# A decoder step on one core: the page loop directly behind the q, k, v projection, unrolled, with the memory projection in its first chunks

## The reference

```python
def sb_block(z, mask, v, carry):
    log_om = jnp.where(mask, jax.nn.log_sigmoid(-z), 0.0)
    suffix = lax.cumsum(log_om, axis=3, reverse=True) - log_om + carry[..., None]
    a = jnp.where(mask, jnp.exp(jax.nn.log_sigmoid(z) + suffix), 0.0)
    o = jnp.einsum("bhqk,bkhd->bqhd", a, v.astype(jnp.float32))
    return o, carry + jnp.sum(log_om, axis=3)

def sb_attention_sample(q, k_new, v_new, cache_k, cache_v, page_table, sb_bias):
    ...
    def page_step(state, phys):                 # 32 pages of 128 keys, newest first
        o_acc, carry = state
        kp = cache_k[phys]
        vp = cache_v[phys]
        zp = sb_logits(q, kp, sb_bias)
        o_p, carry = sb_block(zp, True, vp, carry)
        return (o_acc + o_p, carry), None
    (o, _), _ = lax.scan(page_step, (o, carry), page_table.T, reverse=True)

def memory_kv(mem, g_mem, w_ck, w_cv):          # 256 memory tokens, 1024 -> 512
    mn = rmsnorm(mem, g_mem)
    mk = (mn @ w_ck).reshape(b, N_MEM, CA_HEADS, CA_HEAD_DIM)
    mv = (mn @ w_cv).reshape(b, N_MEM, CA_HEADS, CA_HEAD_DIM)
```

## Time and profile before

| what | value |
|---|---|
| median of 3 runs | 1255.34 us |
| span of the profiled execution (no other time of its own is given) | 1264.7 us |
| TensorE busy in the span | 1122.9 us, 89% |
| VectorE, ScalarE, GpSimd busy | 646.5, 393.0, 405.4 us |
| end of the q, k, v projection on TensorE | 185.3 us |
| page loop, first to last score product | 237.75 to 622.31 us |
| output projection ends | 702.4 us |
| read from HBM | 206.18 MB |

### The profile page before, as it was taken

One profiled execution on the slowest core, in us unless ns is written; L12 is line 12 of the kernel. 1 busy time (PEld: TensorE's weight loads), 2 busy tenths in 40 slices (PEclk: granted clock), 3 DMA queues, 4 the chain that ended last, 5 costly groups with the idle time before them and its releaser, 6 DMA issues.

```text
span 1264.7 us, 27562 instructions
## 1 busy us (share of the span) xinstructions
PE 1122.9 (89%) x10055; PEld 1024.8 (81%) x10055; DVE 646.5 (51%) x890; ACT 393.0 (31%) x609; POOL 405.4 (32%) x327
## 2 busy tenths in 40 slices
PE   5999998789689788788769787899999999999997
PEld 4999997666567566666569775899999999999996
DVE  4214954545455455555579744965455101554444
ACT  6212122345344444444341325321211112121111
POOL 3233334234233333333224101333343434343330
PEclk8999999889799889898879899999999999999998
DMA  6222325999989989989863013322222232322222
GB/s 220 81 87 68 98 68 180 330 377 345 316 296 345 346 288 386 337 301 349 278 212 103 1 67 101 100 68 94 73 69 72 76 107 77 100 66 75 63 63 75
DMA packets 125012, 213.49 MB, mean 169 GB/s; under 512 B 9855, under 2 KB 68412, under 8 KB 124894
## 3 DMA queue, kind: packets, MB, share of 16 engines
q1 hardware_dynamic: 101962, 139.09, 32.6%
q0 software_dynamic: 20480, 67.13, 14.8%
q10 hardware_dynamic: 2452, 5.80, 1.2%
HBM read 206.18 MB, written 5.80 MB: 168 GB/s over the span
## 4 chain that ended last, share of the span: by engine, by line
PE 65%; SPq 9%; DVE 8%; issue 7%; DMA 6%; ACT 3%; POOL 1%; DVEq 0%; ACTq 0%; POOLq 0%
PE ps L453 48%; DMA k_page<-in_cache_sb_k 6%; PE ps L1425 6%; SPq L555 5%; SPq L561 4%; PE ps L519 4%; DVE h_lo L362 3%; PE ps L301 2%; DVE r_sum L616 1%; PE ps L1483 1%; PE ps L1446 1%; POOL w_lo L415 1%; ACT prob L642 1%; DVE r_sq L611 1%; DVE xT L606 1%
## 5 line engine op out<-in xcount | busy, mean ns | idle before, releaser
L415 POOL TENSOR_TENSOR w_lo<-w_raw,w_hi 128x2048 fp32r<-128x2048 f32 (+3 forms) x66 | 267.6, 4056 | 565.0 <-ACT w_hi L391 533.2
L453 PE MATMUL ps<-h_hi,w_hi 128*128 128x288 f32 x1216 | 265.2, 300 | 22.8 <-DVE h_lo L362 19.7
L453 PE MATMUL ps<-h_lo,w_hi 128*128 128x288 f32 x1216 | 262.9, 298 | 0.0
L453 PE MATMUL ps<-h_hi,w_lo 128*128 128x288 f32 x1216 | 262.7, 298 | 0.0
L561 POOL DMA_DIRECT2D v_page<-in_cache_sb_v x256 | 137.7, 538 | 264.8 <-issue 198.7
L391 ACT ACTIVATE w_hi<-w_raw 128x2048 fp32r<-128x2048 f32 (+3 forms) x62 | 106.6, 1723 | 363.6 <-PE ps L453 331.9
L453 PEld LDWEIGHTS ps<-h_hi,w_hi 128*128 128x128 f32 x1216 | 198.6, 191 | 25.4 <-DVE h_lo L362 11.2
L1425 PE MATMUL ps<-cc,k_page 128*128 128x128 f32 x1024 | 149.0, 310 | 62.4 <-DMA k_page<-in_cache_sb_k 38.9
L453 PEld LDWEIGHTS ps<-h_lo,w_hi 128*128 128x128 f32 x1216 | 198.5, 191 | 0.0
L453 PEld LDWEIGHTS ps<-h_hi,w_lo 128*128 128x128 f32 x1216 | 198.4, 191 | 0.0
L1425 PEld LDWEIGHTS ps<-cc,k_page 128*128 128x128 f32 x1024 | 133.8, 161 | 77.8 <-DMA k_page<-in_cache_sb_k 42.2
(11 more groups left out here) (230 smaller groups left out, 1415.2 us busy)
## 6 DMA issues: line engine op xcount, KB each, us to landing
k_page<-in_cache_sb_k SPq DMA_DIRECT2D x256, 256.0 KB, 5.2
v_page<-in_cache_sb_v POOLq DMA_DIRECT2D x256, 256.0 KB, 5.3
w_raw<-in_w_in SPq DMA_DIRECT2D x12, 1024.0 KB, 5.1
w_raw<-in_w_gate SPq DMA_DIRECT2D x11, 1024.0 KB, 5.1
w_raw<-in_w_up SPq DMA_DIRECT2D x11, 1024.0 KB, 5.2
w_raw<-in_w_down SPq DMA_DIRECT2D x8, 768.0 KB, 4.4
w_raw<-in_w_down SPq DMA_DIRECT2D x8, 640.0 KB, 4.0
w_raw<-in_w_out SPq DMA_DIRECT2D x4, 1024.0 KB, 5.3
```

Of the source, the lines that this page charges most:

```text
L415: return nc.gpsimd.tensor_tensor(w_lo[s][:, ks, :], w_raw[s][:, ks, :], w_hi[s][:, ks, :].bitcast(F32), ALU.subtract)
L453: op = nc.tensor.matmul(ps[:, 2 * t + hf, 0:b - a], weights[s][:, k, t * P:(t + 1) * P], x[:, k0 + k, a:b], start=begin and k == ks[0] and ...
```

## The change

The memory projection leaves its place before the loop. Its 8 tiles (`memory_tile`) and 5 row transposes (`memory_rows`) are put into the loop: two before it, two in each of chunks 0, 2 and 3, the rows in chunk 4. Its operands and raw weights get other places, and its conv norm is done by VectorE in chunks 0 to 3. The loop is written out for all 32 chunks on every engine. K has one ring of 8 pages, where a page is loaded as soon as its own slot has been transposed; V has 16, freed page by page. Prompt units begin at chunk 5, one per chunk, with scores behind the sample's scores and transposes and sums in the chunk after. The copies to fixed places go. The weights of a chunk are written over `beta_s`. `c_hi` and `c_lo` are new operands of the output projection, in places that were free in the loop; the place of the ninth and tenth memory block lies in `c_lo`.

The two value blocks now wait for all tiles of the output projection, and the `cq` weights stand behind them. The core of the diff:

```diff
+        v_page = at("v_page", [16, CH], R_H)
+        k_page = at("k_page", [8, CH], R_M)
-        k_page = [at(f"k_page{i}", [8, CH], R_H + i * 16384) for i in range(2)]
-        v_page = [at(f"v_page{i}", [8, CH], R_W + i * 16384) for i in range(2)]
+        def k_pages(sp, C):
+            for q in range(8):
+                if C:
+                    sp.wait_ge(s_ktr, 8 * C + q - 7)
+                load_page(sp, C, q, ck, k_page[:, q:q + 1, :], s_kp[q // 2])
+        def v_pages(pool, C):
+            for q in range(8):
+                slot = 8 * (C % 2) + q
+                if C >= 2:
+                    pool.wait_ge(s_vsum, 8 * C + q - 15)
+                elif slot >= 11:
+                    pool.wait_ge(s_kv_out, 16 * 4)
+                load_page(pool, C, q, cv, v_page[:, slot:slot + 1, :], s_vp[slot // 2])
...
+            k_pages(sp, 0)
+            load_memory_weights(0)
+            load_memory_weights(1)
+            for C in range(1, CHUNKS):
+                k_pages(sp, C)
+                if C in (1, 2):
+                    load_memory_weights(C + 1)
...
+            sp.wait_ge(s_tile["out"], 4 * PAIRS["out"])
             for b in range(2):
                 load_mem(cmv, b, smv_tok[b]).then_inc(s_cmv[0], 16)
             load_stage(sp, "cq")
...
+            memory_lo(0)
+            memory_lo(1)
+            pool.wait_ge(s_tile["in"], 4 * PAIRS["in"])
+            for C in range(CHUNKS):
+                v_pages(pool, C)
+                if C in (1, 2):
+                    memory_lo(C + 1)
...
             def group(g, last):                     # ScalarE
                 for c in range(8):
+                    C, u = 8 * g + c, 8 * g + c - P0
+                    sample_sigmoids(9 * g + c + 1, SEQ)
+                    if 2 <= u < 18 and c:
+                        prompt_out(u - 2)
+                    if C + 1 < CHUNKS:
+                        copy_k(C + 1)
+                    copy_weights(9 * g + c + 1, False)
+                    if 1 <= u < 17:
+                        copy_prompt_weights(u - 1)
+                    if 0 <= u < 16:
+                        prompt_sigmoids(u)
+                    if C in (0, 1):
+                        memory_hi(C + 2)
+                    if C == 4:
+                        memory_rows((0, 2, 4))
+                        store_memory()
...
             def group(g, last):                     # TensorE
                 for c in range(8):
+                    C, u = 8 * g + c, 8 * g + c - P0
+                    if C + 1 < CHUNKS:
+                        k_transposes(C + 1)
+                    if C in (0, 2, 3):
+                        memory_tile((2, None, 4, 6)[C])
+                    if C == 4:
+                        memory_rows((0, 1))
+                    weight_transposes(9 * g + c + 1, 4, u - 1)
+                    if 1 <= u < 17:
+                        prompt_transposes(u - 1)
                     if c < 7:
+                        scores(C + 1)
                     elif not last:
+                        new_scores(g + 1)
+                    if C in (0, 2, 3):
+                        memory_tile((3, None, 5, 7)[C])
+                    if C == 4:
+                        memory_rows((2, 3, 4))
+                    if 0 <= u < 16:
+                        prompt_scores(u)
+                    sums(C)
+                    if 1 <= u < 17:
+                        prompt_sums(u - 1)
...
-            with pe.Fori(0, GROUPS - 1) as g:
-                group(g, False)
-            group(GROUPS - 1, True)
+            for g in range(GROUPS):
+                group(g, g == GROUPS - 1)
```

More of the change, by code:

```diff
@@ new lines, in _ @@
+            split_stage(act, "in", between=lambda: tr_copy(act, even(U_M)), after=bias_and_memory)
+            copied(act, U_M[-1])
+            act.wait_ge(s_sum["conv"], 1)
+            hi_parts(act, "ck", mT, G_MEM, range(KD))
+            memory_hi(0)
+            memory_hi(1)
+            rms_root(act, "conv", rstd_c[:, :], T, CH)
+            nc.scalar.preload_act_table(ACT.Sigmoid)
+            tr_copy(act, even(U_VT))
+            tr_copy(act, even(U_KT))
+            copied(act, U_KT[-1])
@@ new lines, in group @@
+                    weights(9 * g + c + 1, 19 * g + 3 + 2 * c, SEQ)
+                    if C in (1, 3, 4):
+                        evac_memory((3, None, 5, 7)[C - 1])
+                    if C + 1 < CHUNKS:
+                        copy_k(C + 1)
+                    if c == 7 and not last:
+                        queries(g + 1)
+                    if C in (0, 2, 3):
+                        evac_memory((2, None, 4, 6)[C])
+                    if C < 2:
+                        conv_root(C)
@@ L1261, in group @@
+                    if C in (2, 3):
+                        conv_norm(2 * C - 4)
+                        conv_norm(2 * C - 3)
+                    if C == 4:
+                        memory_rows((1, 3))
+                        step(dve, nc.vector.memset(run[:, :, P:SEQ + 1:P], 1.0))
+                    if 1 <= u < 17:
+                        copy_prompt_weights(u - 1)
+                    if 0 <= u < 16:
+                        prompt_weights(u)
                 if not last:
-                    queries(g, 8)
@@ L1272, in group @@
                         op = nc.vector.tensor_copy(
-                            pT[64 * h2:64 * h2 + 64, T_A:T_A + HP, bass.ds(g * 16 + (SEQ + 8 * s), 8)],
+                            pT[64 * h2:64 * h2 + 64, T_A:T_A + HP, SEQ + 16 * g + 8 * s:SEQ + 16 * g + 8 * s + 8],
                             rows[:, :, 16 * s + 8 * h2:16 * s + 8 * h2 + 8])
                 op.then_inc(m_["rows_copied"], 1)
-                if not last:
-                    fix_values(g, 8)
-            queries(0, 0)
-            fix_values(0, 0)
+            queries(0)
             weights(0, 0, NS)
-            copy_k(0, 0)
-            with dve.Fori(0, GROUPS - 1) as g:
-                group(g, False)
-            group(GROUPS - 1, True)
+            lo_parts(dve, "ck", mT, G_MEM, range(KD))
+            copy_k(0)
+            evac_memory(0)
+            evac_memory(1)
+            for g in range(GROUPS):
+                group(g, g == GROUPS - 1)
             grant(s_free["out"], 2)
@@ new lines, in memory_rows, with prompt_scores @@
+            def memory_rows(us):
+                for u in us:
+                    if u < 2:
+                        pe.wait_ge(s_mem_free, 7 + u)
+                    else:
+                        pe.wait_ge(s_mem_ev[u % 2], u // 2)
+                    for j, src in enumerate(mem_units[u][0]):
+                        f = src.shape[-1]
+                        op = nc.tensor.transpose(ps[0:f, 5 + 2 * (u % 2), j * P:(j + 1) * P], src, ident)
+                    op.then_inc(s_mem_tr, 1)
+            def prompt_scores(u):
+                g, qb = divmod(u, NB)
+                if u == 0:
+                    pe.wait_ge(s_mem_ev[0], 3)
+                    pe.wait_ge(s_mem_ev[1], 2)
+                else:
+                    pe.wait_ge(p_["copied_a"], u)
+                    pe.wait_ge(p_["copied_d"], u)
@@ L1513, in group @@
                 if not last:
[L1514 to L1528 removed]
+                    weight_transposes(9 * g + 9, 1, u)
+                    scores(8 * g + 8)
+                    new_sums(g + 1)
+            new_scores(0)
+            k_transposes(0)
+            memory_tile(0)
+            copied(pe, U_KT[-1])
+            weight_transposes(0, 1, 0)
+            scores(0)
+            memory_tile(1)
+            new_sums(0)
+            for g in range(GROUPS):
+                group(g, g == GROUPS - 1)
+            pe.wait_ge(p_["out_copied"], 4 * GROUPS)
             gemm_out(pe)
```

515 lines of the change are left out of this document (229 added, 286 removed).

## The result

| | before | after |
|---|---|---|
| median of 4 runs | 1256.40 us | 1297.70 us |
| lowest and highest | 1253.42 to 1258.08 | 1296.48 to 1303.90 |
| ratio, 95% interval | | 1.033 [1.029, 1.037] |
| profiled execution: span, granted clock | 1264.7, 0.954 | 1294.8, 0.946 |

The change makes the kernel 41 us slower. 1246 us was forecast, with a range of 1220 to 1268.

What follows compares the result with a forecast made beforehand. Pages, TensorE and a ScalarE-VectorE chain were taken to lie within 2 us of one another per step. Loop end -22, low parts +1, query projection +12 gave -9 us: span 1255.7, runs 1246, range 1220 to 1268.

Steps and rivals of the forecast that it cites:

- first scores: Start of the page loop: first score product at 210.4 us instead of 237.75, 27 us earlier.
- steps 0 to 5: Loop steps with the memory tiles: 75 us, plus 4 us for two weight splits on GpSimd.
- steps 6 to 21: Sixteen loop steps with prompt work, prompt scores now behind the sample's: 216 us with two group boundaries.
- steps 22 to 30: Last nine loop steps, no prompt work: set by pages at 10.9 us each, 98 us plus 2 for a boundary.
- last scores to the end of the span: Everything behind the last score product: shorter loop end, 1 us more low parts, 12 us more before cross-attention; 650.7 us.
- median less span: Offset between profiled execution and runs: median 9.4 us below the span, taken over unchanged.
- Rival B: Page loop: K ring of 8 pages closes too late, bringing waits and half clock; 22 us more, 1268; chance 0.20.
- the wait behind the output projection: Before cross-attention's query projection: w_cq weights queue behind memory V loads, nothing hides it; 12 us more, bounds 9 and 15.
- The end of the loop: Last scores to closing products: 8.9 us instead of 13.1, the prompt being done by then.
- A: Steps 6 to 21: TensorE and pages hide the chain, regular steps take 11 us; 25 us less, 1221; chance 0.20.
- the main case: Whole kernel: the summed terms hold, 1246 us with its own range 1235 to 1257; chance 0.48.
- C: Whole kernel: start's gain eaten by GpSimd split stalls and instruction fetch; 8 to 12 us more, 1256; chance 0.12.

Runs made afterwards that it cites:

- e2: Changed kernel with 16 K page slots instead of 8, the second half used by odd chunks from 5 on; 1293.0 us.
- e12: Changed kernel with w_cq weights asked for first, 16 K slots from chunk 7, and prompt scores ahead of the sample's score product; 1247.0 us.
- e6: Changed kernel with w_cq weights first, 16 K slots from chunk 7, and the prompt unit behind the sample's work on ScalarE, VectorE and TensorE; 1255.9 us.
- e3: Changed kernel with the prompt unit's work put behind the sample's on ScalarE, VectorE and TensorE; 1287.1 us.
- e1: Changed kernel with SP asking for the w_cq weights before the two memory V loads that wait for the output projection; 1284.9 us.
- e5: Changed kernel with the prompt's scores ahead of the sample's score product again on TensorE; 1280.5 us.
- e13: Kernel before with straight code and page-wise requests (as e11), but 8 K slots instead of 16; 1277.7 us.
- e11: Kernel before with its loop written out, K and V pages asked for as each slot frees, 16 slots each, K waited for in twos; 1228.0 us.
- e14: Changed kernel with 3 products instead of 24 in each of the eight memory tiles; 1284.4 us.
- e10: Kernel before with its page loop written out on all five engines, nothing else changed; 1241.3 us.
- e9: Kernel before, unedited, profiled once more; span 1253.4 us, one run 1255.1 us.
- e7: Changed kernel with w_cq weights first, 16 K slots from chunk 7, and the 16 prompt units spread over chunks 5 to 30; 1261.8 us.
- e8: As e7, with the prompt unit also behind the sample's work; 1251.3 us.
- e4: Changed kernel without the prompt's attention, page loop and all else kept; 1264.1 us.

## Why the prediction was wrong

The forecast of 1246 missed by 51.7 us. Its own terms:

| step of the prediction | forecast | measured | off |
|---|---|---|---|
| first scores | 210.4 | 213.2 | 2.8 |
| steps 0 to 5 | 78.6 | 86.6 | 8.0 |
| steps 6 to 21 | 216 | 228.9 | 12.9 |
| steps 22 to 30 | 100 | 113.0 | 13.0 |
| last scores to the end of the span | 650.7 | 653.1 | 2.4 |
| median less span | -9.4 | 2.9 | 12.3 |

The rows add up to 51.4; the rest is rounding. The miss is not one error but four of about equal weight and two small ones.

**The step that failed: "without prompt work TensorE needs 8.3, the pages 10.9" (steps 22 to 30, 13.0 us).** The rate of 10.9 a chunk was read from a stretch of the old loop, with 32 slots, and was kept for a kernel with 24. Pages came too late for it: 18.3 us of waits for K pages, at a clock of 0.88. With the eight slots given back the stretch took 95.4 (e2) and 94.6 (e12), below the forecast.

Rival B had this mechanism and was given 0.20 and 22 us. In the changed kernel the ring costs about that: 16 slots bring 18 us (e6 against e3, less e1's 12.8) or 21 (e12 against e5, less the same 12.8). In the old order it costs 44 to 53 (e13 against e11), twice its price. There B's sum fails, 9.7 us a step for 13.0 (404.0 in 31), and not for the landing that it put in: e13's own median, 5.7, gives 10.0. It took every step alike and every page at the median. In e13 steps of 9.3 us stand beside steps of 14 to 18, and behind some of the waits the transposes run at the half clock, which the sum had no term for: over the loop 42 us more of waits than in e11 and 23 us of slower products. That 11.7, the upper end of the earlier trace rows, would have given 13.0 is a match found afterwards and explains nothing.

How many pages were under way can be worked out from rate and landing (medians of K and V pages, half each; estimates). In e11 374 GB/s times 8.2 us is 3.1 MB, 12 pages; in e13 320 GB/s times 5.6 us is 1.8 MB, 7 pages. The kernel before had no more than that with all its 32 slots, 335 GB/s times 5.2 us or 7 pages; it asked for them in blocks of eight, e11 one by one. So it isn't the number of slots alone, but slots and the time of asking together.

**Steps 0 to 5: the size of the pieces, 8.0 us short.** The ring can't be blamed here: TensorE waited 2.4 us for pages. The sum had 4 us for both GpSimd splits; two scans took 4.50 and 4.34 us for 1.27, 6.3 more, within its bounds of 0 to 7. The third step, with the second split and the one page wait in it, took 17.1 for 11.2, the sixth, in which VectorE's scan stood 5.28 us for ScalarE's sigmoids, 16.4 for 13.3. How the rest divides is open; e14 gives no clear answer.

There also lay the hope of the move: the start came 24.5 us earlier, but steps 0 to 5 grew by 22.3 against the first profile. In e12 they took 87.4 against 59.7 in e11, 27.7 more for a start 23.6 earlier. This doesn't show that the memory projection hides nothing, for these steps of e12 have eight slots and those of e11 have 16. With eight slots the old order took 77.5 (e13), 9.9 less than e12 for a start 23.2 later; but it has prompt work in these steps, and e12 has none. Whether the move pays with 16 slots from the first chunk on, no run shows.

**Steps 6 to 21: the mechanism right, the size short by 12.9 us.** The stall from the turned order is there (26.6 us of waits for kT in the stretch), and undoing it gave back 13.5 us (e5). Steps with one, two and three key blocks came as forecast, 11.3, 12.2 and 13.6 for 11.1, 12.2 and 13.5; those of four key blocks took 16.3 to 16.6 for 14.8, 6.6 us in all (behind one of their stalls, of 3.09 us, 16 transposes took 3.09 us, where 2.04 was usual), and the two boundaries with the step behind each took 5 us more. "TensorE's own work, 10.9" was 12.0 (192.5 in 16 steps, granted clock 0.94); in e5 the same work took 11.2 (179.7, at a clock of 0.99). And the order isn't all: with it undone the stretch still took 215.4, as long as was forecast with it. Pages had little part in it: 2.6 us of waits.

**Right in kind and size:** the wait behind the output projection, 12 forecast and 12.8 measured (e1). The same two low parts took 5.15 us beside a GpSimd split and 1.55 without one. The Trainium skill (Advanced Engine Details and Errata, Mode Summary) has VectorE's second SBUF port shared with GpSimd, so that the two can block each other; these rows agree. The end of the loop: 8.9 forecast, 8.5 measured. Nothing is left of waits at the turns; writing out the old loop alone is worth 12.6 us (e10). The Trainium skill (Runtime: NRT & Kernel Launch, Instruction fetch mechanics) says that a taken branch out of the code fetched ahead stops for a fetch; the rows agree with it. In the changed kernel this gain can't be seen apart.

**The offset, 12.3 us.** The prediction took 9.4 us between profile and runs as fixed. e9 shows a span 11.3 lower for the same kernel, and in every later run the time of the profiled execution is 1.7 us above its span: the first profiled execution of before was a slow one. The median was the better base, and a span difference carries the luck of both executions.

**Rivals.** A and the main case are out. B is in for the last stretch, at about its price. C had the sign for part of the loss: the start's gain was eaten, and the splits on GpSimd have a share in it (6.3 us on VectorE); instruction fetch doesn't show. The three repairs give 12.8 (e1), 17.2 (e5) and, for the ring, 18 to 21 us, and together 50.7 (e12), more than the 41 that were lost. What stays open: how the 27.7 us in e12's first steps divide among the ring, the memory tiles, the splits and the two weight loads; and whether the prompt in 16 steps instead of 32 costs e12 its remaining 27 us in S6 to S22, of which S22 to S31 gives 9.7 back. e7 and e8 spread it, but in other orders.

## What to carry to other kernels

Rate times landing time gives the bytes under way, and a slot is only under way between its release and its landing. Before shrinking a ring, shrink it in the kernel that you have and change nothing else, as e13 does: a sum with the median landing time gave 9.7 us a step where the run gave 13.0. Read waits by stretch before naming a cause: here the same kernel waited for copies in one stretch and for pages in the next. Plain improvements of the loop itself (straight code, requests per page, all slots kept) gave 26 us where the large rearrangement lost 41.

## What the runs showed of the hardware

- 256 KB pages moved at 387 GB/s over 59.7 us (e11, S0 to S6), and at 320 over 210.7 us with eight slots fewer (e13, S6 to S22). The Trainium skill (DMA: Bandwidth & Descriptors, Bandwidth) advises transfers of 1 MiB or more for 75% of the peak; these are a quarter of that size.
- Behind a page wait of 2.59 us eight transposes took 1.97 us instead of 1.10, at the lower of TensorE's two clock levels (1.2 GHz); behind one of 0.69 they kept the higher (granted clock 0.50 and 1.00 in the two windows). The mean granted clock of S6 to S22 was 0.99 in e11 and 0.92 in e13. A page that comes late is paid twice.
- Beside a split of 4.5 us on GpSimd a scan on VectorE took 4.50 and 4.34 us, for 1.27 without one.
- How much leaving work out of TensorE shortens the loop depends on what is waited for next: in e14 12.4 us less work gave 2.4 us in S0 to S6, in e4 37.7 us less gave 30.6 in S6 to S22, with waits for pages of 44.0 us for 23.3 over the loop.
